# A decoder step on one core: another order for the opening loads, transposes and weight units

## What is computed

```
def gla_retention_mixer(x, pos, ...):
    z = x @ w_in
    q_g, k_g, v_g, a_lr, r_g, q_r, k_r, v_r, g_r = jnp.split(z, ...)
    log_a = jax.nn.log_sigmoid(a_lr @ w_gate_up + b_gate) / GLA_TAU
    o_g, s_gla = chunked_gated_linear_attention(q_g * GLA_DK ** -0.5, k_g, v_g, log_a, s_gla)
    ...
```

## Time and profile before

| | us |
|---|---|
| median of 3 runs (1363.83 to 1368.92) | 1365.07 |
| the profiled execution, its own time | 1363.26 |
| its span, first to last instruction | 1361.4 |
| PE busy | 1299.1 |

### The profile page before, as it was taken

How to read it: one execution, slowest core, us unless ns; L and a number is a source line. 1 busy time by engine, 2 the same in 40 slices (tenths; PEclk the granted TensorE clock), 3 DMA queues, 4 the chain that set the end, 5 groups by cost and what they waited for, 6 DMA issues and landing times.

```text
span 1361.4 us, 24509 instructions
## 1 busy us (share of the span) xinstructions
PE 1299.1 (95%) x10587; PEld 1281.5 (94%) x10587; DVE 741.0 (54%) x921; ACT 492.8 (36%) x707; POOL 117.2 (9%) x79
## 2 busy tenths in 40 slices
PE   7999999679999999999999999999999999999994
PEld 6999999579899999999998999999999999999993
DVE  3646965856655565653255244458555556642345
ACT  3433235243544434441123333325434344431222
POOL 3000011202300000000012200004100000000023
PEclk9999999789899999999998999998999999999996
DMA  8222204422113132323222222221232323133201
GB/s 262 93 73 84 66 32 128 132 62 90 63 63 122 62 113 72 101 77 116 93 72 77 93 92 92 93 70 57 88 98 75 109 66 119 62 116 117 93 24 63
DMA packets 113395, 121.91 MB, mean 90 GB/s; under 512 B 2529, under 2 KB 108924, under 8 KB 113316
## 3 DMA queue, kind: packets, MB, share of 16 engines
q1 hardware_dynamic: 111492, 115.35, 26.2%
q10 hardware_dynamic: 1632, 5.24, 1.3%
q0 software_dynamic: 208, 0.39, 0.1%
HBM read 114.82 MB, written 6.55 MB: 89 GB/s over the span
## 4 chain that ended last, share of the span: by engine, by line
PE 86%; DVE 5%; ACT 3%; DMA 2%; POOL 2%; SPq 1%; issue 1%; ACTq 0%; DVEq 0%; POOLq 0%
PE ps L363 26%; PE ps L365 26%; PE ps L364 25%; PE ps L570 2%; POOL x_lo L848 1%; PE ps L375 1%; DMA samp_r<-in_state_ret 1%; PE ps L695 1%; ACT x L1181 1%; ACT x_hi L1182 1%; DVE tmp L1579 1%; DVE y_tok L1618 1%; SPq L433 1%; PE ps L378 1%; DMA w_raw<-in_w_mix_in 1%
## 5 line engine op out<-in xcount | busy, mean ns | idle before, releaser
L363 PE MATMUL ps<-x_hi,w_hi 128*128 128x256 f32 (+1 forms) x2144 | 611.2, 285 | 0.0
L365 PE MATMUL ps<-x_hi,w_lo 128*128 128x256 f32 (+1 forms) x2144 | 606.5, 283 | 0.0
L364 PE MATMUL ps<-x_lo,w_hi 128*128 128x256 f32 (+1 forms) x2144 | 604.3, 282 | 0.0
L363 PEld LDWEIGHTS ps<-x_hi,w_hi 128*128 128x128 f32 x2144 | 404.9, 189 | 2.5 <-issue 1.2
L364 PEld LDWEIGHTS ps<-x_lo,w_hi 128*128 128x128 f32 x2144 | 405.9, 189 | 0.1
L365 PEld LDWEIGHTS ps<-x_hi,w_lo 128*128 128x128 f32 x2144 | 404.9, 189 | 0.0
L341 DVE TENSOR_TENSOR w_lo<-w_raw,w_hi 128x2048 fp32r<-128x2048 f32 (+2 forms) x103 | 238.1, 2312 | 224.1 <-ACT w_hi L336 223.8
L336 ACT ACTIVATE w_hi<-w_raw 128x2048 fp32r<-128x2048 f32 (+2 forms) x103 | 192.7, 1870 | 191.3 <-PE ps L365 174.7
L363 PE MATMUL ps<-h_hi,w_hi 128*128 128x264 f32 (+1 forms) x896 | 254.7, 284 | 0.8 <-DVE x L1583 0.8
L365 PE MATMUL ps<-h_hi,w_lo 128*128 128x264 f32 (+1 forms) x896 | 252.7, 282 | 0.0
L364 PE MATMUL ps<-h_lo,w_hi 128*128 128x264 f32 (+1 forms) x896 | 252.7, 282 | 0.0
(11 more groups left out here) (252 smaller groups left out, 1072.5 us busy)
## 6 DMA issues: line engine op xcount, KB each, us to landing
w_raw<-in_w_ffn_in SPq DMA_DIRECT2D x44, 1024.0 KB, 5.0
w_raw<-in_w_ffn_out SPq DMA_DIRECT2D x16, 1024.0 KB, 5.1
w_raw<-in_w_mix_in SPq DMA_DIRECT2D x14, 1024.0 KB, 5.1
w_raw<-in_w_sc_in SPq DMA_DIRECT2D x12, 1024.0 KB, 4.9
w_raw<-in_w_ffn_out SPq DMA_DIRECT2D x8, 768.0 KB, 4.8
w_raw<-in_w_mix_out SPq DMA_DIRECT2D x4, 1024.0 KB, 7.1
w_raw<-in_w_sc_out SPq DMA_DIRECT2D x4, 1024.0 KB, 5.0
x_tok<-in_x_prompt SPq DMA_DIRECT2D x2, 1024.0 KB, 7.5
```

What stands on the lines that cost most here:

```text
L363: e.matmul(out, wh, xh[:, k, lo:hi], start=(first and i == 0), stop=False)
L364: e.matmul(out, wh, xl[:, k, lo:hi], start=False, stop=False)
L365: mm = e.matmul(out, wl, xh[:, k, lo:hi], start=False, stop=(last and i == len(ks) - 1))
```

## The change

Five edits, all in the first 60 us. (1) PE first multiplies a tile of ones by itself ten times, waiting for nothing but the ones. (2) The input is loaded in quarters of 256 features, with unit 0 between the second and the third. (3) The eight k-steps of unit 0 are mixed into the transposes: after the fourth group of transposes PE waits for unit 0's low part and then alternates a k-step with a group. Two of the eight low parts of the input are made by DVE instead of POOL; the high part of unit 0 is staged two tiles earlier, its low part three, and the high part of unit 1 one tile earlier. (4) The first tile of unit 1 comes ahead of the small turns, the second past rows between units 1 and 2, and the first tile of unit 2 ahead of the gate product; the staging of unit 3 is moved ahead of the gate's work on ACT and DVE. (5) SP issues unit 2 ahead of the states and unit 3 ahead of `decay`, and three copies from one DRAM tensor to another after unit 7.

```diff
-            e.dma_start(x_tok[:, 0:4, 0:D // 2], x_rows[:, :, 0:D // 2]).then_inc(load, 16)
+            def load_x(q):
+                d = slice(q * D // 4, (q + 1) * D // 4)
+                e.dma_start(x_tok[:, 0:4, d], x_rows[:, :, d]).then_inc(sem("x_loaded%d" % q), 16)
+            load_x(0)
             e.dma_start(x_tok[0:NS, 4, :], x_sample[:, 0, :]).then_inc(load, 16)
-            e.dma_start(x_tok[:, 0:4, D // 2:D], x_rows[:, :, D // 2:D]).then_inc(sem("x_rest_loaded"), 16)
+            load_x(1)
             load_unit(e, 0)
+            load_x(2)
+            load_x(3)
             load_unit(e, 1)
...
+            e.wait_ge(sem("ones_made"), 1)
+            for i in range(10):
+                e.matmul(bank(0, P, 0, P), ones[:, :], ones[:, :], start=True, stop=True)
...
                 tr.then_inc(sem("x_turned"), 1)
+                if f == 3:
+                    e.wait_ge(lo_made, 1)
+                if f >= 3:
+                    first_step(f - 3)
+            for k in range(KD - 3, KD):
+                mm = first_step(k)
...
+            unit_tile(1, 0)
             e.wait_ge(sem("vec_loaded"), 18 * 16)
...
             turn_past(s_rows0)
-            unit_tile(1, 0)
-            unit_tile(1, 1, [turn_past_1])
+            unit_tile(1, 1)
+            e.wait_ge(sem("past_made"), 2)
+            turn_past(s_rows1)
+            unit_tile(2, 0)
...
             mm.then_inc(sem("gate_summed"), 1)
-            unit_tile(2, 0)
             unit_tile(2, 1)
...
             for f in range(KD):
-                if f == 5:
+                if f == 3:
                     stage_hi(e, 0)
+                if f == 7:
+                    stage_hi(e, 1)
                 e.wait_ge(sem("x_copied"), f + 1)
                 e.activation(x_hi[:, f, :], x32[:, f, :], ACT.Copy).then_inc(sem("x_hi_made"), 1)
-            stage_hi(e, 1)
...
             for f in range(KD):
-                if f == 7:
+                if f == 4:
                     stage_lo(e, 0)
```

More of the change, by code:

```diff
@@ L446, in _ @@
                         ).then_inc(sem("states_loaded"), 16)
+            load_unit(e, 3)
             e.dma_start(decay[:, :], c_decay).then_inc(sem("tables_loaded"), 16)
[L448 to L454, removed]
             e.wait_ge(sem("x_turned"), 8)
@@ L464, in store_rows @@
                             ).then_inc(sem("rows_stored"), 16)
-            for u in range(2, 8):
+            for u in range(4, 8):
                 load_unit(e, u)
+            for l in range(DEPTH):
+                e.dma_start(ffn_s[l, :, 0, :], state_ffn[l, :, 1, :]).then_inc(stored, 16)
+            e.dma_start(conv_s[0, :, 0, :], state_conv[0, :, 1, :]).then_inc(stored, 16)
+            n_stored[0] += 3
             e.wait_ge(sem("past_turned"), 3)
@@ L499, in _, with first_step, unit_tile @@
         def _(e):
-            e.wait_ge(sem("x_loaded"), 48)
+            e.wait_ge(sem("ones_made"), 1)
+            for i in range(10):
+                e.matmul(bank(0, P, 0, P), ones[:, :], ones[:, :], start=True, stop=True)
+            def first_step(k):
+                lo_ready = (sem("x_lo_made"), X_LO_DVE.index(k) + 1) if k in X_LO_DVE else (sem("x_made"), k + 1)
+                return k_step(e, 0, 0, k, x_hi, x_lo, (sem("x_hi_made"), k + 1), lo_ready)
+            e.wait_ge(sem("x_loaded"), 32)
             for f in range(KD):
[L503 to L506, removed]
+                if f % 2 == 0:
+                    e.wait_ge(sem("x_loaded%d" % (f // 2)), 16)
+                if f >= 3:
+                    e.wait_ge(sem("x_copied"), f - 2)
                 for j in range(5):
                     n = P if j < 4 else NS
-                    o = (f % 4) * 1024 + 256 + j * P
+                    o = (1 + f % 3) * 1024 + 256 + j * P
                     tr = e.transpose(ps_t[:, o:o + n], x_tok[0:n, j, f * P:(f + 1) * P], ident[0:n, 0:n])
                 tr.then_inc(sem("x_turned"), 1)
+                if f == 3:
+                    e.wait_ge(lo_made, 1)
+                if f >= 3:
+                    first_step(f - 3)
+            for k in range(KD - 3, KD):
+                mm = first_step(k)
+            mm.then_inc(unit_used, 1)
+            def unit_tile(u, f, pieces=()):
+                if f == 0:
+                    e.wait_ge(lo_made, u + 1)
+                e.wait_ge(acc_free, 2 * u + f - 1)
+                mm_tile(e, u % 2, f, range(KD), x_hi, x_lo, pieces=pieces).then_inc((tile0_done, unit_used)[f], 1)
             e.wait_ge(sem("x_copied"), KD)
[L513 to L516, removed]
+            unit_tile(1, 0)
             e.wait_ge(sem("vec_loaded"), 18 * 16)
@@ L844, in _, with split_x @@
         def _(e):
-            def split_x(f, n):
+            def split_x(f, n, tiles=1):
                 e.wait_ge(sem("x_hi_made"), n)
                 e.tensor_tensor(x_lo[:, f, :], x32[:, f, :], x_hi[:, f, :].bitcast(F32), ALU.subtract
-                                ).then_inc(sem("x_made"), 1)
+                                ).then_inc(sem("x_made"), tiles)
             for f in range(KD):
-                split_x(f, f + 1)
+                if f not in X_LO_DVE:
+                    split_x(f, f + 1, 2 if f - 1 in X_LO_DVE else 1)
             e.memset(hn_stat[:, :, :, :], 1.0).then_inc(sem("cleared_stats"), 1)
```

26 lines of the change are left out of this document (13 added, 13 removed).

## The result

| | before | after |
|---|---|---|
| median, us | 1367.49 (1362.23 to 1371.61, 20 runs) | 1373.64 (1368.10 to 1377.66, 20 runs) |
| ratio to before, 95% interval | 1 | 1.0043 (1.0033 to 1.0054) |
| profiled execution, us | 1363.26 | 1377.07 |
| start of unit 1, of level 0, of level 1, us | 28.66, 62.63, 71.33 | 28.44, 68.31, 81.05 |

The change makes the kernel slower by 0.43%, 6.1 us, where 1365.3 and no change was forecast; 1373.6 lies above the range. The difference is real, since the interval lies wholly above 1, though it is smaller than the half per cent that I had called measurable; twenty runs of each show it.

The account below looks back on a forecast made before the run. PE, with 86% of the chain of waits, bounds the kernel; level 0 comes 1.3 us earlier, lost clock adds 1.5, sum +0.2: 1363.5 profiled, 1365.3 against the median, range 1360 to 1371.5.

Parts of the forecast that it names:

- The start of unit 1: End of the mix on PE: unit 1 starts at 13.0 + 8.4 + 0.455 r, 23.2 us with r = 4.0.
- r: Time in us from the first k-step until TensorE's clock rises; taken as 4.0, each us delaying unit 1 by 0.455.
- The first step: Unit 0's first k-step on PE: at 13.0 us, or 14.7 with transposes at the lower clock, against 19.27 before.
- floor: Unit 1 can't start before 22.9 us: ACT makes its high part at about 18.6, DVE's low part of 2.28 follows.
- From unit 1 to the gate: PE's tiles, small turns, past rows and gate take 22.9 us; the 1.52 us wait for the past rows goes.
- From the gate to level 0: DVE and ACT's chain takes 15.2 us, PE's two tiles 11.6, so PE waits 3.6 us at level 0.
- The clock at level 0: The 3.6 us wait ahead of level 0 costs 1.5 us of clock, ends 0 and 1.8.
- stay low through the mix: Rival: the clock stays low among steps and transposes; r 14.2, level 0 at 66.0, 1370.0 us, or 1371.7; chance 0.25.
- No loss of clock: Rival: the wait at level 0 costs no clock; -1.3 us, 1363.8; chance 0.15.
- no wait at level 0: Rival: the chain behind the gate is shorter or overlaps better, so all 4.9 us count; 1360.2; chance 0.10.
- the quarters don't help: Rival: the input's first quarter lands no earlier than the half did; first step and level 0 move 1.4 us, 1366.7; chance 0.05.
- SP's part at nothing: SP's new issue order, states and tables behind unit 2 and three copies behind unit 7, was costed at nothing.

Follow-up runs that it names:

- e1: Against the changed kernel: old order back behind the new opening (small turns, unit 1, gate, unit 2; staging of unit 3 behind the gate); 1367.21 us, ratio 1.0001.
- e2: Against the kernel before: old opening kept, only the new order behind it and unit 3's staging ahead of the gate's work; 1373.43 us, ratio 1.0048.
- e7: New opening, whole old order behind it, last low part of the input on DVE, SP's states ahead of unit 2; 1361.81 us, ratio 0.9963 to before.
- e9: Against the changed kernel: gate back ahead of unit 2 and last low part of the input on DVE, together; 1363.58 us, ratio 0.9985 to before.
- e5: Against the changed kernel: DVE begins unit 1's low part only when POOL has made all its low parts of the input; one run, 1374.52 us.
- e6: Against the changed kernel: last low part of the input made by DVE, the one before it by POOL; 1367.82 us, ratio 1.0017 to before.
- e3: Against the changed kernel: gate product back ahead of unit 2, second past rows in the midst of unit 1's second tile; 1367.68 us, ratio 1.0001 to before.
- e10: Against e7: the input loaded in halves as before instead of quarters; 1362.29 us, ratio 0.9978 to before.
- e8: Against e7: without the ten products of ones at the start; 1362.05 us, ratio 0.9970 to before.

## Why the prediction was wrong

**The start of unit 1 (23.2, measured 28.44) is the step that failed first.** Of the 5.2 us, 2.19 are the wait for POOL and 1.01 that for ACT. A later rise of the clock, r = 6.5 us where I took 4.0, makes 0.455 x 2.5 = 1.1. The first step gives 0.2 back. Of the 1.1 left, 0.4 are the pairs of a step and a group, each 0.1 longer than the sum of its parts (12.79 to 15.44, 2.65; I had 1.30 + 1.25); the rest I did not trace.

The mistake was in the word floor. I reckoned that unit 1 can't start before 22.9, when DVE has staged it, and asked only who holds up PE from that side. The floor itself was too low: ACT began the high part at 21.51 instead of 18.6, since the seventh tile, which stands ahead of it on ACT, is transposed in the mix only at 19.44, and DVE was through at 25.73. Two questions were missing. What runs beside that staging? POOL's last low part, on which the last k-step hangs. The kernel before had shown the price. There, in its timeline of POOL, DVE's low part of unit 0 (from 16.43 on, 2.18 us) falls into a row of three low parts:

```profile
14.84 4.91 POOL L848 TENSOR_TENSOR x_lo<-x,x_hi 128x520 fp32r<-128x520 f32 x3
```

That is 1.0 us more than three times 1.30. It delayed nothing there that I counted, and I read over it. It also lengthened DVE's own 2.18, which I took as the price of that low part: in e1 it takes 1.22, and there POOL's row of three has 4.80. And what did the small turns cover? I moved them for their own 2.3 us only; at their old place they also hid ACT's copies of unit 0's result, which unit 1 waits for.

**From unit 1 to the gate (22.9, measured 24.6).** The order was right, and the wait at the past rows went, as forecast. The 1.7 are clock: 0.69 and 0.88 in the two stretches behind the waits. In e2, with the wait of 1.01 alone, the clock was 1.00 there. In e7, which has neither wait, it was 1.00, too, but also in e9 behind a wait of 1.74; so the two waits go with the lower clock, and more than that is not shown.

**From the gate to level 0 (15.2 on the chain, 11.6 on PE, an idle time of 3.6).** Right: 53.02 to 68.31 is 15.3, and the idle time is 3.59 in after and 3.58 in e2, e5 and e6, whatever the opening did. In e1 to e3 the loss comes and goes with this wait. It vanishes where the gate goes back (e1, e3).

**The clock at level 0 (1.5, ends 0 and 1.8) is the second term that failed.** From level 0 to level 1 it took 12.74 us in after, 10.26 in e2, 11.74 in e5 and 12.78 in e6, against 8.70: 4.0, 1.6, 3.0 and 4.1 us. My end of 1.8 supposed that the clock rises 4.0 us after level 0 begins. In after it rose 9.0 us after that, and 4.0 us after the matmuls of the next tile began (73.34 to 77.33). Why so late stays open. Level 0's narrower matmuls, on 64 rows, are not reason enough: in e2 the clock fell only after level 0 had begun (granted clock 1.00 up to 67 us, 0.59 from 67 to 68) and was back when the next tile began (0.39 us at 70.68, where after has 0.58 at 73.34), with only those matmuls in between.

**The sum.** 68.31 instead of 61.3 at level 0 makes 7.0, the clock there 2.5 more: 9.5 us of the 13.6 by which the profiled execution missed the 1363.5. The rest lies behind level 1 and is not traced; executions of one kernel differ by more than that (1368.10 to 1377.66 for after). On the medians the miss is 8.3, of which 2.4 is the median of before (1367.49 in the later runs, 1365.07 in those I had).

**The rivals.** The clock did not stay low through the mix; r was 6.5, short of the 6.8 from where that rival decides alone, but past the 3.5 from where it decides together with a loss at level 0. By the prediction's own sum this r would have turned +0.2 into +1.3, so the rest of the loss came by other terms. The nine kernels with the mix and the ones had r at 3.4 to 6.5, the one without the ones at about 9. In three of the nine (e1, e5, e6) the first step still ran at the upper level (0.51 us instead of 0.80) and the clock fell behind it; that the steps begin at the lower level was not certain, either. Had the rule on transposes from the Trainium skill, TensorE: Matmul & The Clock Gate, Part 4: PE-mode transpose, held for the mix as well, the clock would not have risen there: it did, in every run. No loss of clock and no wait at level 0 were both wrong. That the quarters don't help was wrong: e10 shows 1.5 us at the first step. The low chance for clearly slower (0.08) came from having each loss alone among the rivals: the wait at level 0 was certain by my own rows, and a rival in which its clock loss and the opening's misses come together was never priced.

**SP's part at nothing** was right for after, where a tile stands ahead of the small turns, and wrong as soon as they come early: 2.14 us in e1. **The ten products** I had counted for the first step's 13.0 instead of 14.7; without them it stood at 13.57, since what it waits for is unit 0's low part (2.66 us in e7 and e8 alike), not the transposes.

## What to carry to other kernels

An operation that is moved ahead leaves its old place bare: list what it covered there before pricing what it saves, and what its new neighbours share with it, as POOL and DVE do when both read two tiles. On a path where two engines are within a few microseconds of each other, a chain shortened by 2.2 us is worth nothing when the work beside it is shortened by 5.8; read both sides up to the point where they meet. A wait ahead of busy TensorE work costs its length and, in these executions, between nothing (1.01 us in e2, 1.74 in e9) and a little more than that again in clock (4.1 for 3.58 in e6), so a wait that is taken from one place and put at another can well be a loss.

## What the hardware showed that I had not expected

- POOL's subtraction of 128x520 elements took 2.80 us beside DVE's subtraction of two SBUF tiles and 1.28 to 1.32 alone, and ended 1.14 to 1.15 us after DVE, in after, e1 and e3 alike. At unit 0, where DVE's subtraction (128x1024) falls among three of POOL's, either can be the longer one: 1.74 us and 3.78 in after, 1.22 and 4.80 in e1.
- An idle time of 3.58 to 3.59 us behind work at the full clock, in one execution each of four kernels, cost between 1.6 and 4.1 us of clock. A price for one wait has to be a range.
- The same wait of 1.74 us ahead of unit 1 left the clock at 1.00 in e9 (28 to 32 us) and at 0.66 in e6. The two kernels have the same order up to there; why they differ stays open.
